# Modulation rows of the delta rule's first block pair: from VectorE's running total to TensorE row products

## The reference

```python
c_act = jax.nn.silu(c)
mod = c_act @ ada_w[i] + ada_b[i]                       # (2048) @ (2048, 12288)
sh1, sc1, g1, sh2, sc2, g2 = jnp.split(mod, 6, axis=-1)
h = x * (1.0 + sc1) + sh1
proj = h @ w_in                                         # layer 0: q, k, v, z, b, a, u
ya = gated_deltanet(q, k, v, z, b, a, ...)
yb = s5_ssm(u, ...)                                     # 32 diagonal state tiles, then a gate: y * sigmoid(y @ w_glu)
x = layer_norm(ALPHA * x + (1.0 + g1) * (concat([ya, yb]) @ w_out))
```

## Time and profile before

| | |
|---|---|
| median of 3 runs | 2767.47 us (2767.14 to 2772.09) |
| profiled execution | 2774.95 us, of it 2773.3 us span |
| PE busy | 2546.4 us (92%) |
| DVE busy | 2046.8 us (74%) |
| ACT busy | 1220.2 us (44%) |
| steps 4 to 31 of the stage | 223.1 to 464.3 us of the span |

### The profile page before, as it was taken

The page is one execution under the profiler, slowest core; times in us unless marked ns, Lnnn a source line. Parts: engine busy times, 40 slices in busy tenths (PEclk is TensorE's granted clock), DMA queues, the critical chain, the costliest instruction groups (busy, mean ns, idle before and its releaser), DMA issues.

```text
span 2773.3 us, 41862 instructions
## 1 busy us (share of the span) xinstructions
PE 2546.4 (92%) x16532; PEld 2303.7 (83%) x16532; DVE 2046.8 (74%) x2486; ACT 1220.2 (44%) x1614; POOL 202.1 (7%) x226
## 2 busy tenths in 40 slices
PE   1499998888889999999999899998999999999998
PEld 1488777777878899889988799998878998899887
DVE  8879999777487777777778887568887655545556
ACT  1255555543455433443343453453463434443444
POOL 0013332000000000000001011000000000000000
PEclk8589999888899999999999899999999999999998
DMA  9874444555448888887888499556578656555652
GB/s 375 283 252 146 150 150 147 195 174 198 136 139 295 275 275 281 281 272 274 278 281 288 154 316 334 184 168 221 189 272 283 214 190 194 185 193 184 195 185 77
DMA packets 272987, 616.02 MB, mean 222 GB/s; under 512 B 23211, under 2 KB 23746, under 8 KB 272578
## 3 DMA queue, kind: packets, MB, share of 16 engines
q1 hardware_dynamic: 240020, 488.00, 51.9%
q0 software_dynamic: 32640, 125.84, 13.1%
q10 hardware_dynamic: 174, 0.04, 0.0%
HBM read 611.73 MB, written 2.10 MB: 221 GB/s over the span
## 4 chain that ended last, share of the span: by engine, by line
PE 75%; DVE 16%; DMA 3%; issue 2%; ACT 2%; SPq 2%; DVEq 0%; POOL 0%; POOLq 0%
PE groups L2533 11%; PE groups L2537 11%; PE groups L2535 11%; PE groups L2541 10%; PE groups L2543 10%; PE groups L2545 10%; DMA ada_units<-in_ada_w_dram 3%; DVE ada_acc L2033 2%; DVE w_lo L2051 1%; PE pc L2712 1%; SPq L1660 1%; DVE s_zm L2448 1%; PE pb L2702 1%; DVE ada_acc L873 1%; DVE ada_acc L2358 1%
## 5 line engine op out<-in xcount | busy, mean ns | idle before, releaser
L1750 ACT ACTIVATE w_hi<-w_raw 128x1024 fp32r<-128x1024 f32 x776 | 817.3, 1059 | 1139.5 <-PE groups L2537 545.9
L2051 DVE TENSOR_TENSOR w_lo<-w_raw,w_hi 128x1024 fp32r<-128x1024 f32 x747 | 905.4, 1223 | 532.1 <-ACT w_hi L1750 528.2
L2533 PE MATMUL groups<-w_hi,act_hi 128*128 128x512 f32 x1408 | 554.1, 394 | 20.0 <-DVE act_lo L2185 20.0
L2535 PE MATMUL groups<-w_hi,act_lo 128*128 128x512 f32 x1408 | 550.5, 391 | 0.0
L2537 PE MATMUL groups<-w_lo,act_hi 128*128 128x512 f32 x1408 | 550.4, 391 | 0.0
L2541 PE MATMUL groups<-act_hi,w_hi 128*128 128x256 f32 x1776 | 512.7, 289 | 37.1 <-DVE act_lo L2185 14.2
L2543 PE MATMUL groups<-act_lo,w_hi 128*128 128x256 f32 x1776 | 504.3, 284 | 0.0
L2545 PE MATMUL groups<-act_hi,w_lo 128*128 128x256 f32 x1776 | 503.9, 284 | 0.0
L2541 PE MATMUL groups<-hid_hi,w_hi 128*128 128x256 f32 x1392 | 390.4, 280 | 0.0
L2545 PE MATMUL groups<-hid_hi,w_lo 128*128 128x256 f32 x1392 | 388.7, 279 | 0.0
L2543 PE MATMUL groups<-hid_lo,w_hi 128*128 128x256 f32 x1392 | 388.7, 279 | 0.0
(11 more groups left out here) (437 smaller groups left out, 2500.4 us busy)
## 6 DMA issues: line engine op xcount, KB each, us to landing
ada_units<-in_ada_w_dram POOLq DMA_DIRECT2D x120, 1024.0 KB, 6.8
w_raw<-in_ffn_w_gate_dram SPq DMA_DIRECT2D x88, 1024.0 KB, 5.2
w_raw<-in_ffn_w_up_dram SPq DMA_DIRECT2D x88, 1024.0 KB, 5.3
w_raw<-in_ffn_w_down_dram SPq DMA_DIRECT2D x88, 1024.0 KB, 5.2
w_raw<-in_cd_w_in_dram SPq DMA_DIRECT2D x48, 1024.0 KB, 5.9
w_raw<-in_ab_w_in_dram SPq DMA_DIRECT2D x40, 1024.0 KB, 6.0
ada_units<-in_ada_w_dram SPq DMA_DIRECT2D x80, 512.0 KB, 4.5
w_raw<-in_ab_w_out_dram SPq DMA_DIRECT2D x16, 1024.0 KB, 5.9
```

What stands on the lines that cost most here:

```text
L1750: act.activation(whi[:, half, k], raw[:, slot, k], ACT.Copy).then_inc(hi_done, 1)
L2051: dve.tensor_tensor(wlo[:, half, k], raw[:, slot, k], whi[:, half, k].bitcast(F32), ALU.subtract).then_inc(lo_done, 1)
L2533: pe.matmul(dst, hi[:, k, rows], whi[:, j % 2, kk], start=(k == 0), stop=False, skip_group_check=True)
L2535: pe.matmul(dst, lo[:, k, rows], whi[:, j % 2, kk], start=False, stop=False, skip_group_check=True)
```

## The change

The 16 modulation operations of the first pair leave DVE. In their place PE makes 32 products, in eight calls of `ada_rows` with four products each: a slice's 128 values of `c_act`, repeated over 32 columns, are the stationary operand (128x32), and half a slice (128x512) is the moving one. The four products of a call (two slices, two halves) go to the four 32-partition parts of the bank `pm`, and each part is summed over the eight calls. A call stands behind the 48 products of the *second* step of each pair in `EARLY_AT`: in steps 5, 11, 13, 19, 21, 27, 29 and 31, ahead of `s5_out`. The semaphore (now `dn_ada_used`) grows by two with the last product of a call. ACT copies the bank to `ada_acc` (`ada_row_copy`), and `ada_sum(0)` turns the rows to columns with eight small products, which replace the eight of before.

```diff
@@ deltanet_ada_load
             if m > 3:
-                sp.wait_ge(dn_ada_dve, m - 3)
+                sp.wait_ge(dn_ada_used, m - 3)
@@ deltanet_act
             squares(0)
             side_split(0)
+            ada_row_copy(act)
             rows_g(0)
@@
+        def ada_rows(pe, pair_of_slots):
+            first, last_pair = pair_of_slots == 0, pair_of_slots == KT // 2 - 1
+            if first:
+                pe.wait_ge(mod_taken, glu["ab1"] + 1)
+            for a in range(2):
+                m = 2 * pair_of_slots + a
+                pe.wait_ge(dn_ada_in[m % 4], 16 * (m // 4 + 1))
+                for half in range(2):
+                    rows = slice(64 * a + 32 * half, 64 * a + 32 * half + 32)
+                    last = pe.matmul(pm[rows], cact[:, m:m + 1].broadcast_to([P, 32]),
+                                     ada_slot(m)[:, GROUP * half:GROUP * half + GROUP], start=first, stop=last_pair)
+            last.then_inc(dn_ada_used, 2)
+
+        def ada_row_copy(act):
+            act.wait_ge(dn_ada_used, KT)
+            act.activation(acc[:, 0], pm[:], ACT.Copy).then_inc(dn_row_taken, 1)
 
         def deltanet_early_dve(dve, n):
-            if n in EARLY_AT:
-                ada_op(dve, EARLY_AT.index(n))
@@ ada_sum
-                if pair:
-                    on(dnd, f"take{pair - 1}")
-                else:
-                    pe.wait_ge(mod_taken, glu["ab1"] + 1)
-                pe.wait_ge(dn_ada_dve, KT * (pair + 1))
+                if pair == 0:
+                    pe.wait_ge(dn_row_taken, 1)
+                    for t in range(GT):
+                        for a in range(2):
+                            last = pe.matmul(pm[:, t:2 * GT:GT], acc[:, 0, P * t:P * t + P], ident[:, 64 * a:64 * a + 64:32],
+                                             start=(a == 0), stop=(a == 1), skip_group_check=True)
+                    done(last, f"ada{pair}")
+                    return
+                on(dnd, f"take{pair - 1}")
+                pe.wait_ge(dn_ada_used, KT * (pair + 1))
@@ s5_after (PE)
                 n = 8 * i + j
+                if n in EARLY_AT[1::2]:
+                    ada_rows(pe, EARLY_AT.index(n) // 2)
                 s5_out(n)
```

More of the change, by code:

```diff
@@ L402, in build @@
         dn_ada_in = [sem(f"dn_ada_in{n}") for n in range(4)]
-        dn_ada_dve = sem("dn_ada_dve")
+        dn_ada_used, dn_row_taken = sem("dn_ada_used"), sem("dn_row_taken")
         level_masks = sem("dn_level_masks")
@@ L871, in ada_op @@
             else:
-                dve.wait_ge(dn_ada_dve, n)
+                dve.wait_ge(dn_ada_used, n)
                 last = dve.scalar_tensor_tensor(total, unit, cact[:, k:k + 1], total, ALU.mult, ALU.add)
-            last.then_inc(dn_ada_dve, 1)
+            last.then_inc(dn_ada_used, 1)
+        def ada_rows(pe, pair_of_slots):
[13 more added lines that the diff above has]
+            act.activation(acc[:, 0], pm[:], ACT.Copy).then_inc(dn_row_taken, 1)
         def deltanet_early_dve(dve, n):
-            if n in EARLY_AT:
-                ada_op(dve, EARLY_AT.index(n))
             if n in CONV_AT:
```

## The result

| | before | after |
|---|---|---|
| median | 2768.84 us (2767.14 to 2772.09, 4 runs) | 2790.2 us (2784.51 to 2792.23, 4 runs) |
| ratio | | 1.0071, interval 1.0056 to 1.0086 |
| profiled execution | 2774.95 us, span 2773.3 | 2789.36 us, span 2787.7 |
| steps 4 to 31 (starts of tiles 4 and 31) | 223.13 to 459.23: 236.10 us | 221.36 to 474.76: 253.40 us |

The changed kernel is slower by 0.71%, 19.7 us by the ratio of the runs (21.4 by the two medians), where 21.2 were forecast. The forecast total was close. Several of its terms were not, and the experiments take them apart.

The account below looks back on a forecast made before the run. DVE was taken to set the pace, with PE close behind at 8.12 us a step. Terms -16.6 + 15.1 - 1.2 + 21.0 + 1.9 + 1.0 = +21.2 us, set on the median 2767.47, gave 2788.6 us, range 2775 to 2800.

Parts of the forecast that it names:

- DVE's relief: Steps 4 to 30 and behind the last tile: time above PE's 8.12 us a step goes with DVE's modulation operations, -16.6 us.
- seven calls, less the hidden part: Seven PE calls of 2.15 us, +15.1; in steps 11, 19 and 27 about 0.4 each falls into PE's existing wait, -1.2.
- three stops and the slow clock: Ahead of units 12, 20 and 28: loads stuck behind slice loads cost 7.0 us each, +21.0; half clock behind them, +1.9.
- copy and `ada_sum(0)`: At `ada_sum(0)` PE waits for ACT's copy, which stands behind a half of `w_hi`: +1.0 us.
- rival (b): A call's four products run all side by side, 0.95 us a call, 8.4 less: 2780.2 us; chance 0.18.
- (a): A call's products run one behind the other, 3.44 us a call: 2798.8 us; chance 0.27.
- (c): Unit 12 comes in time, so loads don't stop PE: 2758.5 us, or 2765.8 with calls of 2.15; chance 0.08.
- (d): The change doesn't relieve DVE, so the 16.6 us are not gained; chance 0.02.
- (1): SP's queue waits for PE; loads of units 12, 20, 28 issue just behind products of units 11, 19, 27.
- (5): A call's four products span 2.15, 0.95 or 3.4 us, which tells the forecast from its rivals on call price.
- (2): PE has three idle stretches of 5 to 6 us, released by `w_lo`; steps 12, 20, 28 begin 7 us late.
- (4): Steps without a stop and without a call run at 8.12 to 8.5 us.

Follow-up runs that it names:

- no_modulation_work: Kernel before, with modulation operations 2 to 16 of the first pair cut to one column each on DVE: 2753.57 us, ratio 0.9943.
- loads_behind_use: Changed kernel with the loads of slices 4 to 15 queued on SP in pairs, behind units four steps after the freeing call: 2763.26 us, ratio 0.9979.
- one_column_part: Changed kernel with slice loads queued behind their use, plus all four products of a call on the same 32 columns: 2774.13 us, ratio 1.0021.
- single_slices: Changed kernel with one slice a call, two products in each of the sixteen steps where DVE's operation stood: 2763.49 us, ratio 0.9973.
- early_copy_alone: Changed kernel with only ACT's copy of the bank moved, to between the first two parts of the last gelu: 2781.28 us, ratio 1.0047.

## Why the prediction was right in the sum and wrong in two terms

Each term is the difference of two kernels or of two places, and together they make up the stretch but for 0.1 us:

| term | predicted | measured | how |
|---|---|---|---|
| DVE's relief | -16.6 | -16.0 | no_modulation_work: 243.85 - 259.86 |
| seven calls, less the hidden part | +15.1 - 1.2 = +13.9 | +5.3 | steps 4 to 31: loads_behind_use 226.43, no_modulation_work 221.16 |
| three stops and the slow clock | +21.0 + 1.9 = +22.9 | +27.0 | steps 4 to 31: changed kernel 253.40, loads_behind_use 226.43 |
| copy and `ada_sum(0)` | +1.0 | +4.1 | `glu` to `pa<-dn_rows,ones`: 17.60 - 13.47 |
| sum | +21.2 | +20.2 | 0.1 less between tile 31 and `glu`, rounding |

**The relief: right.** The count of each step's time above 8.12 held, to 0.6 us in 16. Of the 0.6, the first operation is 0.25 (no_modulation_work keeps it whole), and 0.26 lies behind the last tile, where 1.07 came back and not 1.33.

**The calls: mis-sized.** The step that failed is "PE starts products in order", from which I took it that the first record of a product starts only beside the second record of the one ahead of it. I priced a call at 2.15; it costs 0.87. In the trace four first records lie side by side and then four second ones, 1.06 us for all eight. A product on other columns doesn't wait for the first record of the one ahead of it. one_column_part shows the same from the other side, and so does single_slices, where the S5 products on a part of their own run beside the call. The price was that of rival (b), which was given 0.18 and should have had the most. The Trainium skill (TensorE: Matmul & The Clock Gate, Part 3: packing small matmuls) gives the span of such packed products as the time of one and about 4 ns for each further one. By that rule, the trace agrees: 0.87 us for four, against 0.86 for one of the same 512 columns on all of them. Rival (b)'s time, 2780.2, missed only because it kept the other terms.

**The stops: right, and a little dearer.** Place, number and mechanism are as predicted: slice 6 behind PE's call, unit 12 behind slice 6, three times. PE could start 8.93 us behind the call (8.6 predicted), since the transfer took 6.04 and each conversion a little longer. It was idle for 6.62 (5.9), also because the S5 products ahead of that took 2.3 and not 2.7. The tile of step 12 began 10.22 behind the call, as the 10.2 of the prediction. Measured, a stop is 7.8 against a call step without one; 0.4 of it is the hidden part, which a stop takes away again and which I had credited with -1.2. Left are 7.4 against 7.0.

**The clock: mechanism right, size uncertain.** Predicted +1.9; in the changed kernel 3.4 us were lost (3.1 in its second profile), and with idle products in the stops 3.5 came back. In early_copy_alone the same steps lost 1.4, so the prediction's size lies inside what executions show. The loss was 1.7 us behind the first stop and less behind the others (steps of 9.83, 9.25, 8.63), where I had taken one size, less what the late tile hides, for all three.

**The copy: mis-sized by the same mechanism.** I saw the wait (+1.0, measured 2.28) and not that it would bring the low clock with it. The wait itself grew by the clock ahead of it: PE comes to `ada_sum(0)` 5.71 us behind the first `glu` product (491.85 - 2.28 - 483.86), where it had been 7.18. The kernel before had a low clock of its own at `glu`, behind 3.72 us of idle. The relief alone doesn't take that away: in no_modulation_work the idle time is 2.34 us and the way to `pa<-dn_rows,ones` still 13.47.

```profile
454.32 0.52 PE L1134 MATMUL groups<-act_hi,w_hi 128*128 128x256 f32 x1 [2.34 <-DVE act_lo L891]
```

In the changed kernel the eighth call fills part of this gap too and 1.25 is left; with the early copy the result is seen: 11.85 us in place of 13.47. So the copy costs 5.75 us, and 4.1 net of that.

**The sum** came out within 1 us because -8.6 for the calls, +4.1 for stops and clock, +3.1 for the copy and +0.6 for the relief nearly cancel. The forecast can claim the stops, the relief and the sign; that it came within 1 us was luck.

**The rivals.** (a) is out: even where the products do run in a line, a call costs 2.15, since the S5 products run beside it. (c) is out by its own deciding point: a unit issued behind the call needs 8.9 us, and the S5 products give 2.3. Its arithmetic without the stops, faster by 9.0 us with side by side products, is close to the -6.7 that loads_behind_use showed; most of the difference is the copy's 4.1 for 1.0. (d) is out by the wait of 0.7 us. **The signs** (1) and (5) came as written. (2) came in kind, but PE's idle stretches are 6.6 us and not 5 to 6, and steps 12, 20 and 28 begin 7.8 late rather than 7; by the prediction's own last sentence it was wrong in the size of a stop. (4) holds but for steps 12, 20 and 28 themselves, which the low clock stretches to 9.83, 9.25 and 8.63. (3) was a poor sign: DVE's share fell to 40.21 of 50 us only because everything stands still in a stop; without stops it is 47.68.

**Open.** The rows show that the clock falls behind 2.28 us of idle at `ada_sum(0)`, and behind 2.34 and 3.72 ahead of `glu`, but not behind 1.25 ahead of `glu`. Why the one gap and not the others, what part the work ahead of a gap has, and why the low clock behind equal stops lasts longer in one execution than in another, wasn't tried.

## What to carry to other kernels

Where a load waits until something is used, everything behind it on the same issuing queue waits too: a change that makes the use later, or moves it to another engine, has to move the load as well, or the lead of all the other transfers is lost. Price a wait ahead of TensorE by the time until the next point that both kernels reach, not by its own length, since the clock behind it can cost more than the wait. And where the executions scatter by more than the effect, compare a short stretch between two fixed instructions, and confirm it by a control that differs in one thing.

## What the runs showed of the hardware

- Four f32 products of 128x32 by 128x512 on four different column parts take 0.87 us a call, one on all columns 0.86. The records run as four firsts and four seconds, eight in 1.06 us.
- Two such products cost 0.87 us where the S5 products behind them use one of their column parts, and nothing where those use another: in single_slices they start at 236.16 and 236.17.
- A product on one column part starts while records of products ahead of it in PE's queue, on another part, haven't started: 308.92 for the first `pc` record, 309.34, 309.77 and 310.20 for the last three of the call.
- The granted clock fell to 0.50 behind a wait of only 2.28 us, and the way to the next common point was 5.75 us longer by it. Three stops of 6.6 us, filled with products that nobody needs, kept it at 1.00 and gave 3.5 us back; behind the same stops unfilled, 1.4 to 3.4 us were lost in different executions.
